# Two attentions of a two-block diffusion layer: row maxima, sums and reciprocals rearranged

## The reference

```python
scores = q @ k.T * scale            # 1280 keys (256 context, then 1024 latent)
probs  = softmax(scores, axis=-1)   # exp(score - row maximum) / sum
out    = probs @ v                  # branch attention: times its gate
```

## Time and profile before

| | |
|---|---|
| time, median of 3 (lowest, highest) | 4682.5 us (4680.52, 4684.68) |
| the profiled execution: its time | 4677.3 us |
| its span, first to last instruction | 4675.5 us |
| mean granted clock of TensorE | 0.921 of full speed |
| PE, DVE, ACT, POOL busy | 85%, 59%, 42%, 20% of the span |
| first branch attention | from about 293 to 491 us |
| second branch attention | from about 1355 to 1534 us |
| latent attention | from about 2310 to 3107 us |

### The profile page before, as it was taken

How to read it: one execution, slowest core, us unless ns; L and a number is a source line. 1 busy time by engine, 2 the same in 40 slices (tenths; PEclk the granted TensorE clock), 3 DMA queues, 4 the chain that set the end, 5 groups by cost and what they waited for, 6 DMA issues and landing times. The chain is left out here.

```text
span 4675.5 us, 58731 instructions
## 1 busy us (share of the span) xinstructions
PE 3961.6 (85%) x22208; PEld 3036.3 (65%) x22208; DVE 2742.5 (59%) x4041; ACT 1986.3 (42%) x3646; POOL 956.4 (20%) x1088
## 2 busy tenths in 40 slices
PE   7978888987978787977788888869979797999898
PEld 5755667876764675666455555547756676888686
DVE  4754467966754567855544444434977574566545
ACT  4533264544543265344333333324544353444344
POOL 0015003600005002500044444430037000111100
PEclk7988899989988898988889999989989898999999
DMA  4100113654100111041000000022000542111243
GB/s 167 37 14 1 51 46 118 218 186 139 37 19 1 51 37 46 2 153 39 27 5 5 9 5 5 1 83 59 28 6 1 203 157 82 48 43 55 77 144 140
DMA packets 211274, 297.08 MB, mean 64 GB/s; under 512 B 74090, under 2 KB 139882, under 8 KB 210996
## 3 DMA queue, kind: packets, MB, share of 16 engines
q1 hardware_dynamic: 210436, 293.14, 18.7%
q0 software_dynamic: 416, 0.05, 0.0%
q10 hardware_dynamic: 144, 0.15, 0.0%
HBM read 262.17 MB, written 31.03 MB: 63 GB/s over the span
## 5 line engine op out<-in xcount | busy, mean ns | idle before, releaser
L500 DVE TENSOR_TENSOR x_low<-buf_a,x_high 128x1280 fp32r<-128x1280 f32 (+4 forms) x384 | 376.3, 980 | 433.9 <-ACT x_high L469 430.7
L526 PE MATMUL ps<-x_high,w_high 128*128 128x512 f32 (+1 forms) x1344 | 496.7, 370 | 101.1 <-DVE w_low L504 96.2
L469 ACT CAST x_high<-buf_a 128x1280 fp32r<-128x1280 f32 (+4 forms) x384 | 327.7, 853 | 579.3 <-PE ps L528 494.4
L527 PE MATMUL ps<-x_low,w_high 128*128 128x512 f32 (+1 forms) x1344 | 484.3, 360 | 0.0
L528 PE MATMUL ps<-x_high,w_low 128*128 128x512 f32 (+1 forms) x1344 | 484.1, 360 | 0.0
L2935 PE MATMUL ps<-w_high,x_high 128*128 128x512 f32 x896 | 364.3, 407 | 95.3 <-DVE w_low L2778 91.6
L526 PEld LDWEIGHTS ps<-x_high,w_high 128*128 128x128 f32 x1344 | 259.1, 193 | 173.0 <-DVE x_low L500 112.9
L2936 PE MATMUL ps<-w_low,x_high 128*128 128x512 f32 x896 | 357.9, 399 | 0.0
L2937 PE MATMUL ps<-w_high,x_low 128*128 128x512 f32 x896 | 357.4, 399 | 0.0
L2778 DVE TENSOR_TENSOR w_low<-w,w_high 128x1024 fp32r<-128x1024 f32 x170 | 208.0, 1223 | 194.5 <-ACT w_high L2891 194.5
L3433 DVE TENSOR_REDUCE mx<-ps 128x1 fp32r<-128x1280 f32 x128 | 190.9, 1492 | 218.2 <-PE ps L3305 217.5
(11 more groups left out here) (446 smaller groups left out, 9098.1 us busy)
## 6 DMA issues: line engine op xcount, KB each, us to landing
w<-in_w_out SPq DMA_DIRECT2D x26, 2048.0 KB, 8.8
w<-in_w_mod SPq DMA_DIRECT2D x24, 2048.0 KB, 9.2
w<-in_w_down SPq DMA_DIRECT2D x15, 2048.0 KB, 7.7
w<-in_w_in SPq DMA_DIRECT2D x26, 1024.0 KB, 5.1
w<-in_w_up SPq DMA_DIRECT2D x22, 1024.0 KB, 7.5
w<-in_w_in SPq DMA_DIRECT2D x7, 2048.0 KB, 8.5
x<-in_x SPq DMA_DIRECT2D x16, 512.0 KB, 9.4
scratch_branches<-buf_b SPq DMA_DIRECT2D x4, 1280.0 KB, 5.6
```

The source lines that it names most:

```text
L469: act.copy(xh[i % NX][:, 0:s["tn"]], x_of(s)).then_inc(x_high, 1)
L500: dve.tensor_tensor(xl[i % NX][:, 0:s["tn"]], x_of(s), xh[i % NX][:, 0:s["tn"]].bitcast(F32), ALU.subtract).then_inc(x_low, 1)
L526: pe.matmul(g["out"], lhs[0][:, :], rhs[0][:, :], start=(s["kk"] == 0), stop=False)
L527: pe.matmul(g["out"], lhs[0][:, :], rhs[1][:, :], start=False, stop=False)
```

## The change

- **Row maxima.** Both attentions make one row score per key step: 0, 2, 4, 6 and 7 ahead of the scores of steps 1, 3, 5, 7 and 8; 1, 3 and 5 behind those of steps 2, 4 and 6. In unit 0, odd row scores use banks 5 to 7, so that PE writes one set while DVE reads the other.
- **Sums.** ACT copies the sums out of PSUM (`sums_out`, step 2), which frees the bank; DVE inverts the copy in pieces of 128 columns, one per step, from step 4 (branch: 3), and multiplies at step 9 (`finish`).
- **Late sums.** DVE adds the tiles of steps 8 and 9 straight to the unit's sum, four adds in place of two, and POOL's two are gone. DVE waits until POOL's adds are done.
- **Queries' low parts** (in the branch also the keys') go from DVE to POOL, between its adds.
- **Latent attention, start:** constant rows go mostly to POOL, the first pair's groups take banks 3 and 4 in turn, and the low rope rows come after the fourth maximum. The second set of constant rows is copied at unit 1.
- **Branch attention:** the first unit of 512 queries of the first key head becomes two of 256. The first unit's row scores use the high parts alone (64 rows), so that they need no low keys. ACT casts in another order and spreads the next unit's queries over steps 0 and 1.

```diff
-             for g in range(2) for t0, tn in LAT_BLOCKS]
+             for g in range(2) for t0, tn in ([(CTX, CTX), (2 * CTX, CTX), (CTX + HALF, HALF)] if g == 0 else LAT_BLOCKS)]
...
-    ADDS = 2 * EARLY
+    ADDS = 2 * (EARLY - 1)
-    ENDS = [0, 1, 2, 4, 5, 6, 8, 8, 8, 8]
+    BEFORE, AFTER = {1: 0, 3: 2, 5: 4, 7: 6, 8: 7}, {2: 1, 4: 3, 6: 5}
+    def row_bank(u, r):
+        return 5 if u == 0 and r % 2 else 0
...
+        place(("group", 0, g), 3 + g % 2)
...
-            pe.wait_ge(inverted, jobs[n][1] + 1)
+            pe.wait_ge(copied, first[1] + 1)
...
+                if u == 1:
+                    pool.wait_ge(added, n)
+                    for s in range(2):
+                        constant_rows(1, s)
...
+                    if u + 1 < U and i in (2, 4):
+                        pool.wait_ge(added, n)
+                        queries_low(u + 1, i // 2 - 1)
+                        pool.wait_ge(q_low, 2 * (u + 1) + i // 2)
...
-                for s in range(2):
-                    pool.wait_ge(late_done, 2 * u + s + 1)
-                    pool.wait_ge(added, n - 1)
-                    pool.tensor_tensor(acc[u % 2][s][:, :], acc[u % 2][s][:, :], late[s][:, :], ALU.add).then_inc(added, 1)
...
-                if g >= 1:
+                if u >= 1:
                     pe.wait_ge(maxed, g)
+                elif r >= 2:
+                    pe.wait_ge(maxed, r - 1)
...
             for n, (u, i) in enumerate(STEPS):
+                for r in rows_at(u, i, BEFORE):
+                    row_scores(u + 1, r)
                 for s in range(2):
                     scores(u, i, s)
+                for r in rows_at(u, i, AFTER):
+                    row_scores(u + 1, r)
                 for p, g in groups_at(u, i):
                     group(p, g)
-                for r in rows_at(u, i):
-                    row_scores(u + 1, r)
...
+            def sums_out(u):
+                act.wait_ge(summed, u + 1)
+                if u >= 2:
+                    act.wait_ge(normed, u - 1)
+                act.copy(rec[u % 2][:, :], ps[:, bank("sum", u), :]).then_inc(copied, 1)
...
-                    dve.tensor_tensor(late[s][:, :], pt[a % NPT], pt[b % NPT], ALU.add).then_inc(late_done, 1)
+                for j in range(2):
+                    for s in range(2):
+                        m, a = tile_no(u, EARLY + j, s), acc[u % 2][s][:, :]
+                        dve.wait_ge(exped, m + 1)
+                        if j == 0:
+                            dve.wait_ge(added, ADDS * (u + 1))
+                        else:
+                            dve.wait_ge(late_done, 2 * u + s + 1)
+                        dve.tensor_tensor(a, a, pt[m % NPT], ALU.add).then_inc(late_done if j == 0 else totals, 1)
...
-                dve.reciprocal(rec[:, :], ps[:, bank("sum", u), :]).then_inc(inverted, 1)
+            def invert(u, c):
+                dve.wait_ge(copied, u + 1)
+                part = rec[u % 2][:, c * P:(c + 1) * P]
+                dve.reciprocal(part, part).then_inc(inverted, 1)
...
+                if u and 4 <= i < 4 + NQ:
+                    invert(u - 1, i - 4)
+                if u and i == KEYS - 1:
+                    finish(u - 1)
```

More of the change, by code:

```diff
@@ L3404, in _ @@
                         pairs.evacuate(act, p, g, bank("group", p, g))
+                    if i == 2 and u:
+                        sums_out(u - 1)
+            sums_out(U - 1)
         @block.vector
         def _(dve):
[L3408 to L3425, removed]
             def maxima(u, r):
@@ L3466, in _ @@
                     add_late(u - 1)
-                if i == 3 and u:
-                    normalise(u - 1)
+                for r in rows_at(u, i, BEFORE) + rows_at(u, i, AFTER):
+                    maxima(u + 1, r)
                 for p, g in groups_at(u, i):
@@ L3520, in adds @@
     def adds(u):
[L3522 removed]
+        return 2 * (early(u) - 1)
     a0 = [0]
@@ L3530, in rows_at, with row_bank, parts @@
         if u + 1 >= U:
-            return []
+            return [], []
         rows = r0[u + 2] - r0[u + 1]
         if steps_of[u] < LONG:
-            return [2 * i, 2 * i + 1]
-        ends = [0, 1, 2, 4, 5, 6, 8, 8, 8, 8] if rows == 8 else [0, 1, 2, 3, 4, 4, 4, 4, 4, 4]
-        return list(range(ends[i - 1] if i else 0, ends[i]))
+            return [], [2 * i, 2 * i + 1]
+        before, after = {1: 0, 3: 2, 5: 4, 7: 6, 8: 7}, {2: 1, 4: 3, 6: 5}
+        return [r for j, r in before.items() if j == i and r < rows], [r for j, r in after.items() if j == i and r < rows]
+    def row_bank(u, r):
+        return 5 if u == 0 and r % 2 else 0
+    def parts(u):
+        return range(0, units[u]["nq"], P)
     def row_place(u, r):
@@ L3596, in _ @@
                         n += 1
-                if steps_of[u] == LONG:
-                    for s in range(2):
-                        pool.wait_ge(late_done, 2 * u + s + 1)
-                        pool.wait_ge(added, n - 1)
-                        a = acc[u % 2][s][:, 0:units[u]["nq"]]
-                        pool.tensor_tensor(a, a, late[s][:, 0:units[u]["nq"]], ALU.add).then_inc(added, 1)
-                        n += 1
+                    if u + 1 < U and i == (5 if steps_of[u] == LONG else 1):
+                        pool.wait_ge(added, n)
+                        for s in range(2):
+                            queries_low(u + 1, s)
+                            pool.wait_ge(q_low, 2 * u + s + 3)
         @block.tensor
@@ L3660, in _ @@
             for g, (u, i) in enumerate(STEPS):
+                before, after = rows_at(u, i)
+                for n in before:
+                    row_scores(u + 1, n)
                 for s in range(2):
                     scores(u, i, s)
-                for n in rows_at(u, i):
+                for n in after:
                     row_scores(u + 1, n)
@@ L3688, in queries, with sums_out @@
                 act.copy(q_two[u % 2][s][HD:P, 0:w["nq"]], w["q"][s]).then_inc(q_high, 1)
-            keys(units[0]["kid"])
+            def sums_out(u):
+                w = units[u]
+                act.wait_ge(summed, u + 1)
+                if u >= 2:
+                    act.wait_ge(normed, u - 1)
+                act.copy(rec[u % 2][:, 0:w["nq"]], ps[:, bank("sum", u), 0:w["nq"]]).then_inc(copied, 1)
             queries(0, 0)
+            keys(0)
             queries(0, 1)
-            keys(1 - units[0]["kid"])
+            keys_again(0)
@@ new lines, in _ @@
+            for g, (u, i) in enumerate(STEPS):
+                w = units[u]
+                if u + 1 < U and i < 2:
+                    queries(u + 1, i)
+                for s in range(2):
+                    m = tile_no(u, i, s)
+                    act.wait_ge(st_ready, m + 1)
+                    if m >= NPT:
+                        uu, ii = STEPS[(m - NPT) // 2]
+                        act.wait_ge(pv_done, s0[uu] + ii + 1)
+                        if ii < early(uu):
+                            act.wait_ge(added, a0[uu] + 2 * (max(ii, 1) - 1) + s + 1)
+                        else:
+                            act.wait_ge(totals, 2 * uu + s + 1)
+                    act.activation(pt[m % NPT][:, 0:w["nq"]], ps[:, bank(u, i, s), 0:w["nq"]], ACT.Exp, scale=scale
+                                   ).then_inc(exped, 1)
+                if g % 2 == 0 and g >= 2 and STEPS[g - 2][1] == 0 and STEPS[g - 2][0] >= 1:
+                    sums_out(STEPS[g - 2][0] - 1)
+                    summed_out += 1
@@ L3755, in normalise, with add_late @@
-            def normalise(u):
-                w = units[u]
-                r = rec[:, 0:w["nq"]]
-                dve.wait_ge(summed, u + 1)
+            def add_late(u):
+                nq = units[u]["nq"]
+                for j in range(2):
+                    for s in range(2):
+                        m, a = tile_no(u, LONG - 2 + j, s), acc[u % 2][s][:, 0:nq]
+                        dve.wait_ge(exped, m + 1)
+                        if j == 0:
+                            dve.wait_ge(added, a0[u + 1])
+                        else:
+                            dve.wait_ge(late_done, 2 * u + s + 1)
+                        dve.tensor_tensor(a, a, pt[m % NPT][:, 0:nq], ALU.add).then_inc(late_done if j == 0 else totals, 1)
```

289 lines of the change are left out of this document (156 added, 133 removed).

## The result

The changed kernel takes 4444.18 us (median of 4 runs, 4442.71 to 4444.85) where the kernel before takes 4683.59 in the same session (4680.52 to 4685.54). The ratio is 0.9489, with a 95% interval of 0.9473 to 0.9505: 239 us faster. The profiled execution took 4442.71.

What follows compares the result with a forecast made beforehand. PE sets the pace, held by waits for row maxima and the reciprocal. Terms sum to -244, less allowances -226: from 4677.3 to 4451.3, plus 5.2 for the runs' median, so 4457 us; range 4436 to 4532.

Steps and rivals of the forecast that it cites:

- The latent attention: Units 0 to 13 at 75.6 us a pair, -150; with unit 14, unit 15, tail and start, -166 in all.
- about half of what lies beyond the idle time is clock: Whole kernel: low PE clock makes up about half the loss beyond idle time; dense work should hold 2.4 GHz.
- The start of the stage: Latent attention's start: last maximum 6 us earlier, unit 0's wait already in the pairs, so only -1 us.
- The row maxima: Latent attention: tightest row scores 2.7 us apart, above the 2.49 us cycle, so PE does not wait for maxima.
- The reciprocal: Sums' bank comes free after a copy of some 0.6 us, not 3.35; pieces of 0.84 fit between two maxima.
- The branch attentions: Start, small units, full units, last 512 unit and end together give -38 and -40 us, before allowances.
- full units: Branch attention's units of 512 queries: 27.6 us each, with 1.25 for the landing; -12.6 and -11.1.
- end: Branch attention, first layer: context units wait for copy, four pieces and two multiplies, +1.5 us.
- rival 1: The clock does not come back: short waits keep it falling, only idle time goes, -152, 4530 us; chance 0.12.
- rival 2: Another queue (ACT, POOL or DVE) holds PE, 3 us in each of 16 + 8 units; 4530 us; chance 0.13.
- The third: Small units cost less or the allowances are not needed: -244, 4438 us; chance 0.12.
- rival 4: Slower: late maxima's DMAs land late at some 23 unit borders, deciding at 9.8 us each; chance 0.02.

Runs made afterwards that it cites:

- single columns: The changed kernel with SP sending each column of maxima as soon as its own maximum is done, not four at once: 4415.61 us, ratio 0.9424.
- the old order: The changed kernel with row scores back in their old places, in both attentions; copy and pieces stay: 4594.87 us, ratio 0.9808.

## Why the prediction was right, and where it was off

- **The latent attention** is right term by term, but for its start. The 14 units with projections take 529.6 us, 75.6 a pair, the forecast to a tenth, though partly by chance: pairs are 74.8, and unit 0's idle 6.0 us make up the rest. The full clock was counted on, and came: 1.00 in every unit from 1 to 14, with PE busy for 397 of 400 us. The Trainium skill (TensorE: Matmul & The Clock Gate, What's actually happening) has it that activity releases the throttled state; the trace agrees, with that 1.00. The runs above add that the clock does not follow from the idle time alone. The prediction's "about half of what lies beyond the idle time is clock" is hard to check as it stands; undoing the order of the maxima gave 9.0 us of idle time and 8.4 beyond it in a pair.
- **The start of the stage** was the term most undersized: -10.4 for -1. I had the last maximum 6 us earlier and set unit 0's wait against it; it is 10.4 earlier (it starts 29.5 us after the stage's start, 39.9 before). Unit 0 did keep a wait of 4.4 for the DMA, but that is in the 529.6 already, so the gain stands whole.
- **The row maxima.** The spacing held against the 2.49 us of the cycle: 0.4 us of wait remains in every other unit, none in the rest. The wait for the DMA at unit borders, put at 0.1 to 0.3 us, is under 0.1 in the latent attention.
- **The reciprocal**: the step was right that the copy ends the wait for the bank. The pieces were booked at 0.84 us and take 0.94 where they stand apart. In the latent stage one long reciprocal does as well, so the argument that the pieces must fit between two maxima was not needed there.
- **The branch attentions** gave 28.5 and 34.0 for 37.7 and 40.2. The start was met: the second head's first scores at 305.88 for 307, which is 20.1 of the 20 forecast when the stage's own start, 1.0 earlier, is taken off. So were the small units, 19.3 and 22.3 us for 16 and 25, and the first full unit at 344.5 for 348. What was off first are the full units, "27.6" for 29.8: the landing was put at 1.25 us and is 2.96 and 1.5, and the clock is 0.94 in them. The sum had them at 1.00; with single columns they run at 1.00 and take 26.4. In branch 1 they take 31.3 and 27.8. What was off more is the **end** of branch 0, "+1.5": it is +7.2. There the four late adds on DVE wait for POOL and stand in front of a maximum that PE wants (timeline, branch 0, 426 to 433):

```profile
429.70 2.50 DVE L3833 TENSOR_TENSOR acc<-acc,kt 128x512 f32<-128x512 f32 x4 [8.43 <-POOL acc L3662]
...
432.11 0.42 DVE L3821 TENSOR_REDUCE mx<-ps 128x1 fp32r<-128x256 f32 x1
...
432.68 0.55 PE L3691 MATMUL ps<-k_low_high,q_high_twice 128*128 128x256 f32 x1 [3.71 <-DVE mx L3821]
```

  DVE stands idle for 8.43 us until POOL's adds are done, the late adds take 2.50, and PE's row score waits 3.71 us for the maximum behind them. In the kernel before DVE added `pt` to `pt` there, waiting for no one on POOL. With the adds on POOL the part took 29.9 us, so they account for 4.9 of the 7.2. I had costed the copy and the pieces of that end, and not the adds' new wait with the maximum queued behind it. In branch 1, without context units, the last part gave 2.6 us where I had 6.5. Of the missing 3.9, a landing takes 1.2, and the last sums 0.9, since they ran at the low clock (1.98 us for 1.08); the rest is not accounted for.
- **The rivals.** The clock that does not come back (rival 1) did not happen in the latent attention; in the full branch units it came back in part, and the old order shows it to be a real price. The queues that hold PE (rival 2) showed only in that end. The third, -244, comes nearest. The forecast lies 13 us above the result, because I took allowances from both stages where the latent attention needed none, and for the 4 us named above. Its total is also closer than its parts: the start's 9 us too little and the branch attentions' 15 too much partly cancel, and that is luck. The landing (rival 4) did cost, 29 us by the kernel with single columns, far from the 9.8 us a border at which it would decide.

## What to carry to other kernels

Look for the engine that is waiting for a round trip (row score, maximum, next row score) and put other ready work of that engine between two rounds: here taking the new order of the row maxima out again cost 151 of the 239 us. Read idle time as a lower bound, since waits of 1.7 us went with a lower clock for the work around them in some units and not in others, and test a spread order before an operation is cut into pieces, because slack can make the pieces needless, as in the latent attention here. Before shrinking the first unit to start sooner, count what the small units cost in waits for their own borders.

## What was not expected of the hardware

- With the old order PE's granted clock was 0.91 though PE was busy for 358 of 400 us; with one wait of 1.7 us in a unit it was 0.99 at 381 busy, with four it was 0.94 at only 333. Like units with like waits ran at 0.92 and at 1.00.
- A reciprocal on DVE takes 0.94 us for 128 columns, 1.76 for 256 and 3.35 for 512. Four pieces apart take 3.77 us, but on end they take 3.39 (447.65 in branch 0's end), hardly more than one.
- SP takes 2.4 us to issue the four DMAs of one head's maxima when they come at once; sent as each maximum is done, they saved 29 us over both kinds of attention, most of it in the branch ones (by the stages of the profiles 10.3 and 9.5, and 5.1 in the latent).
